# Hybrid decoder trunk, Mamba-2 mixer: gates, norm sums and the first decode rows at later units

## The chip, the cores and the metric

The kernel runs on one core of a Trainium2 chip. The metric is the device time of one execution in microseconds; lower is better. A core has TensorE (matmuls; PE, and PEld for its weight loads), VectorE (DVE), ScalarE (ACT), GpSimd (POOL) and SyncE (SP), each with a queue of its own that it works off in order. Semaphores tie the queues together.

## What is computed

One inference step of a two-layer decoder for a prompt of 256 tokens and 8 decode requests with one token each, which share all weights. The first layer is a half-SwiGLU, a Mamba-2 mixer, a half-SwiGLU and a gated per-layer embedding; the second has windowed attention in place of the mixer. The change touches only the mixer:

```python
def mamba2_mixer(u, w_in, conv_w, conv_b, dt_bias, a_log, d_skip, norm_g, w_out, ssm0, conv0):
    z, xbc, dt_raw = jnp.split(u @ w_in, [D_INNER, D_INNER + CONV_DIM], axis=-1)
    conv = conv_b + sum(xbc_full[:, k:k + t_len] * conv_w[k] for k in range(CONV_W))
    xs, bm, cm = jnp.split(silu(conv), ...)
    y, h_last = ssd_scan(xs, dt, a, bm, cm, ssm0)
    y = y + d_skip * xs
    gated = y * silu(z)                                  # 2048 channels in 8 groups
    gg = gg * rsqrt(mean(gg * gg, over the group) + EPS)
    out = (gg * norm_g) @ w_out
```

## The kernel before

The 264 columns (256 prompt tokens, 8 decode tokens) lie along the free dimension of every tile, features on the 128 partitions. The weights are cut into units of 128 x 1024 values. SP loads them into a ring of four; ACT rounds each to a high part (L982), DVE takes the rest as a low part (L1395), and TensorE makes three products for each of 8 tiles (L435 to L437), 24 matmuls for a unit.

The mixer's input projection has 49 units, numbered s_ = 0 to 48 (list SIN): one for dt, 16 for z, 32 for the convolved channels. Every engine's program runs over the same slots s_ = 0 to 51 (SLOTS), and the lists at L95 to L104 say in which slot a small step is issued. On TensorE the small matmuls of a slot come behind the unit of that slot, in the order of the loop at L870 to L896: add_inter, decode_rows, chunk_in and chunk_out, norm_sums, decode_columns. Each engine only waits for semaphores, so a step's slot is its place in the queue, not a time.

For each of the 8 groups g:
- The scan runs in two chunks of 128 tokens. CHUNK_AT[g] gives the slot. chunk_in (L756, L757) makes the differences of which ACT takes the exponential (L1173, with a table load), DVE multiplies (L1739), chunk_out (L770, L775, L777) uses the product.
- decode_rows (L796) spreads a state row over partitions; ACT copies them (copy_rows, L1180); decode_columns (L811, L813), one slot later, turns them; DVE reads them two slots after the rows (decode_read, L1699 and L1701); POOL finishes (dec_outputs, L2050).
- In slot GATE_AT[g] DVE multiplies y by silu(z) (gate, L1759) and ACT squares it (L1239). In slot NORM_AT[g] POOL adds the two tiles of squares (pair_squares, L2056) and TensorE sums them over the partitions into bank 2 (norm_sums, L827).
- In slot ROOT_AT[0] = NORM_AT[3] ACT takes the square root of the first four groups' sums (L1245, semaphore gated_std); in the next slot DVE inverts it (invert_stats, L1764); two and three slots after the root POOL sends it to DRAM and back, spread over the partitions (stats_out, stats_in). It is used from slot APPLY_AT = 43 on.

Inside a slot, DVE's order is: take the unit from PSUM (L1442), decode_read, the three convolution taps of the unit before (L1643), steps of the chunk, gate, low part of a later unit; in slots without a chunk the low part comes ahead of these; then invert_stats. ACT's order is: high part of a later unit, first tap (L1139), exponential, SiLU of the unit before (L1145 or L1150), copy_rows, square, root.

Decode columns and norm sums write into different columns of PSUM bank 2, from which DVE (decode_read) and ACT (the root) read. The waits in norm_sums and decode_columns keep TensorE from writing while the others read: norm_sums(g) waits until all decode_reads are done whose columns lie in an earlier slot than NORM_AT[g]; decode_columns waits for the root where it comes behind it.

Of the kernel before, what the change touches and what calls it, by code (L numbers as in the profile page):

```python
# [95 lines left out]
DEC_CONV_AT = [e_ + 1 for e_ in LAST_CONV]  # L96
DEC_SILU_AT = [e_ + 2 for e_ in LAST_CONV]
DEC_PROD_AT = [14] + [e_ + 3 for e_ in LAST_CONV[1:]]
DEC_AT = [16, 19, 23, 27, 32, 37, 43, 46]
GATE_AT = [19, 22, 26, 30, 36, 46, 48, 50]  # L100
NORM_AT = [t_ + 1 for t_ in GATE_AT]
ROOT_AT = [NORM_AT[3], NORM_AT[7]]
APPLY_AT = 43
SLOTS = ROOT_AT[1] + 1  # L104
# [44 lines left out]
def trunk_kernel(nc, weights, xT, pT, cst, vec, convst, ssm0, kcT, vc_in, ck, cv,  # L149
# [3 lines left out]
    with ExitStack() as ctx:  # L153
# [275 lines left out]
        def _(pe):  # L429
# [306 lines left out]
            def chunk_in(k):  # L736
# [14 lines left out]
                if c == 1:  # L751
                    pe.wait_ge(dec_copied, [d_ < CHUNK_AT[g] + 1 for d_ in DEC_AT].count(True))
                if k == 0:
# [5 lines left out]
            def chunk_out(k):  # L759

                g, c = k // 2, k % 2
                yb = bank[6]
                pe.wait_ge(ssd_mm, k + 1)
                if k == 0:
                    pe.wait_ge(pre_a, 3)
                if g >= 1 and c == 0:
                    pe.wait_ge(ssd_y, g)

                for h in range(4):
                    pe.matmul(yb[64 * (h % 2):64 * (h % 2) + 64, 256 * (h // 2) + 128 * c:256 * (h // 2) + 128 * c + 128],  # L770
                              xdt[k % 2][:, 64 * h:64 * h + 64], Dm[k % 2][:, 128 * h:128 * h + 128],
                              start=h < 2, stop=c == 0, skip_group_check=True)
                if k > 0:
                    pe.wait_ge(ssd_carry, k)
                mm = pe.matmul(bank[3][:, 0:256], cbb[k % 2][:, 128:256], xte[k % 2], start=True, stop=True)  # L775
                if c == 1:
                    mm = pe.matmul(bank[3][:, 256:512], xact[:, 24 + g, 128:256], h1, start=True, stop=True)  # L777
                mm.then_inc(ssd_part, 1)

            def add_inter(g):  # L780

                pe.wait_ge(ssd_isc, g + 1)
                for n_ in range(2):
                    mm = pe.matmul(bank[6][:, 256 * n_ + 128:256 * n_ + 256], isc[:, 128 * n_:128 * n_ + 128], ident,
                                   start=False, stop=True, skip_group_check=True)
                mm.then_inc(ssd_tr, 1)

            def decode_rows(g):

                pe.wait_ge(h0_landed[H0_BUF[g]], 16 * h0_turn(g))  # L790
                pe.wait_ge(dec_act, g + 1)
                pe.wait_ge(ssd_exp, 2 * [c_ + 1 < DEC_AT[g] for c_ in CHUNK_AT].count(True))
                if g > 0:
                    pe.wait_ge(dec_copied, g)
                for q in range(SEQS):
                    mm = pe.matmul(bank[7][32 * (q % 4):32 * (q % 4) + 32, 256 * (q // 4):256 * (q // 4) + 256],  # L796
                                   dact[:, g, 1, q:q + 1].to_broadcast([P, 32]), h0buf[H0_BUF[g]][:, 256 * q:256 * q + 256], start=True, stop=True)
                mm.then_inc(h0_used, 1)

            def decode_columns(g):  # L800

                pe.wait_ge(dec_copied, g + 1)
                pe.wait_ge(dec_prod, g + 1)
                if g > 0:
                    pe.wait_ge(dec_read, g)
                if DEC_AT[g] + 1 > NORM_AT[3]:
                    pe.wait_ge(gated_std, 1)
                c_ = N + 24 * g
                for i in range(2):
                    for t in range(2):  # L810
                        pe.matmul(bank[2][:, c_ + 8 * t + 4 * i:c_ + 8 * t + 4 * i + 4], crow[:, 256 * i + 128 * t:256 * i + 128 * t + 128],  # L811
                                  ident[:, 0:P:32], start=True, stop=True)
                pe.matmul(bank[2][:, c_ + 16:c_ + 24], ones, bc_d[:, g, :], start=True, stop=True).then_inc(dec_sel, 1)  # L813

            def norm_sums(g):

                if g < G - 1:
                    pe.wait_ge(gated_pair, g + 1)
                else:
                    pe.wait_ge(gated_sq, G)  # L820
                pe.wait_ge(dec_read, [d_ + 1 < NORM_AT[g] for d_ in DEC_AT].count(True))
                if g >= 4:
                    pe.wait_ge(gated_std, 1)
                rows = bank[2][32 * (g % 4):32 * (g % 4) + 32, 0:N]
                tiles = 1 if g < G - 1 else 2
                for k in range(tiles):
                    mm = pe.matmul(rows, ones[:, 0:32], gsq[:, k, :], start=k == 0, stop=k == tiles - 1)  # L827
                mm.then_inc(gated_sum, 1)
# [42 lines left out]
            for s_ in range(len(SIN)):  # L871
                if s_ == 1:
                    unit_pair("sin", 0)
                elif s_ > 1:
                    sin_unit(s_)
                if s_ == PRE_AT:
                    pre_tokens()
                if s_ == PRE_AT + 3:
                    pre_sums()
                for g in range(G):  # L880
                    if s_ == CHUNK_AT[g] + 3:
                        add_inter(g)
                if s_ in DEC_AT:
                    decode_rows(DEC_AT.index(s_))
                for g in range(G):
                    if s_ == CHUNK_AT[g]:
                        chunk_in(2 * g)
                    if s_ == CHUNK_AT[g] + 1:
                        chunk_in(2 * g + 1)
                        chunk_out(2 * g)  # L890
                    if s_ == CHUNK_AT[g] + 2:
                        chunk_out(2 * g + 1)
                if s_ in NORM_AT:
                    norm_sums(NORM_AT.index(s_))
                if s_ - 1 in DEC_AT:
                    decode_columns(DEC_AT.index(s_ - 1))  # L896
# [78 lines left out]
        def _(act):  # L975
# [190 lines left out]
            def decay_exp(k):  # L1166

                if k + 1 < 2 * G:
                    select(k + 1)
                act.wait_ge(ssd_diff, k + 1)  # L1170
                if k >= 2:
                    act.wait_ge(ssd_part, k - 1)
                act.activation(Dm[k % 2], bank[5 + 2 * (k % 2)][:, 0:512], ACT.Exp).then_inc(ssd_exp, 1)  # L1173
# [22 lines left out]
            for s_ in range(SLOTS):  # L1196
# [35 lines left out]
                if s_ in CHUNK_AT[1:]:  # L1232
                    decay_exp(2 * CHUNK_AT.index(s_))
                if s_ in GATE_AT:
                    g = GATE_AT.index(s_)
                    act.wait_ge(gated, g + 1)
# [152 lines left out]
        def _(dve):  # L1389
# [331 lines left out]
            def carry(k):  # L1721

                g, c = k // 2, k % 2
                dve.wait_ge(ssd_part, k + 1)
                if c == 0:
                    dve.tensor_copy(h1, bank[3][:, 0:256]).then_inc(ssd_carry, 1)
                    return
                if g > 0:
                    dve.wait_ge(ssd_tr, g)
                dve.tensor_tensor(by_head(isc), by_head(bank[3][:, 256:512]), heads(tok[:, 1, 0, 4 * g:4 * g + 4]), ALU.mult).then_inc(ssd_isc, 1)  # L1730
                link(dve, dve_step, steps, dve.tensor_tensor(by_head(h1), by_head(h1), heads(tok[:, 1, 2, 4 * g:4 * g + 4]), ALU.mult))
                if g >= 2:
                    dve.wait_ge(st_out[g % 2], 16 * (g // 2))
                dve.tensor_tensor(state[:, g % 2, :], h1, bank[3][:, 0:256], ALU.add).then_inc(ssd_carry, 1)
# [19 lines left out]
            def gate(g):  # L1754

                dve.wait_ge(z_silu, 2 * g + 2)
                dve.wait_ge(dec_y, g + 1)
                dve.wait_ge(ssd_y, g + 1)
                dve.tensor_tensor(zs[:, 2 * g:2 * g + 2, :], zs[:, 2 * g:2 * g + 2, :], xact[:, 2 * g:2 * g + 2, :], ALU.mult).then_inc(gated, 1)  # L1759
# [11 lines left out]
            for s_ in range(SLOTS):  # L1771
# [36 lines left out]
                for g in range(G):  # L1808
# [7 lines left out]
                    if s_ == CHUNK_AT[g] + 2:  # L1816
                        carry(2 * g + 1)
                if s_ in GATE_AT:
                    gate(GATE_AT.index(s_))
                if s_ < len(SIN) and chunks:  # L1820
# [159 lines left out]
        def _(pool):  # L1980
# [72 lines left out]
            def pair_squares(g):  # L2053

                pool.wait_ge(gated_sq, g + 1)
                pool.tensor_tensor(gsq[:, 0, :], gsq[:, 0, :], gsq[:, 1, :], ALU.add).then_inc(gated_pair, 1)  # L2056
# [11 lines left out]
            for s_ in range(SLOTS):  # L2068
                if s_ in NORM_AT[:G - 1]:
                    pair_squares(NORM_AT.index(s_))  # L2070
# [251 lines left out]
```

## Time and profile before

| | us |
|---|---|
| median of three runs | 1239.3 |
| lowest and highest | 1239.04, 1241.94 |
| the profiled execution | 1243.26 |
| span of the profiled execution | 1241.2 |

| engine | busy us |
|---|---|
| TensorE, matmuls | 1206.5 |
| DVE | 885.1 |
| ACT | 689.8 |
| POOL | 233.1 |

The span is the time from the first to the last instruction of the profile. "Busy" counts the time in which an engine has an instruction in work. Idle time of an engine that isn't the bottleneck costs nothing; what counts is where TensorE stands still, and which wait ends last there.

### The profile page before, as it was taken

The page shows a single profiled execution, that of the slowest core. Times are in us where ns is not written, and L with a number is a line of the kernel's source. Part 1 is how long each engine was busy: PE and PEld are TensorE (multiplying, and loading weights), DVE is VectorE, ACT ScalarE, POOL GpSimd, SP SyncE. Part 2 cuts the span into 40 slices and gives each one's busy share as a digit, 9 for nine tenths or more (in the row PEclk, how much of TensorE's full clock was granted, in tenths as well). Part 3 has the DMA queues.
Part 4 walks back from the last instruction along what each step waited for, and adds up shares of the span by engine and source line. Part 5 has one row for each costly group of instructions (what it writes and reads, how often), then busy time and mean ns, then how long its engine had stood idle before and what let it go on. Part 6 is the DMA issues. An engine that isn't in the chain of part 4 may idle for free.

```text
span 1241.2 us, 26732 instructions
## 1 busy us (share of the span) xinstructions
PE 1206.5 (97%) x9875; PEld 1172.5 (94%) x9875; DVE 885.1 (71%) x1405; ACT 689.8 (56%) x1098; POOL 233.1 (19%) x338
## 2 busy tenths in 40 slices
PE   6999999899999999999999999999999999999998
PEld 6999999888888889999999999999998899999998
DVE  5666646987888777786744988788469758776447
ACT  6444436676576547556555764555357656445335
POOL 0000002312222111132344333332015310000001
PEclk9999999999999999999999999999999899999999
DMA  7655554644443445857686666756743135455552
GB/s 265 230 207 182 185 178 153 227 157 177 143 158 134 149 136 189 333 193 278 242 316 224 213 239 222 263 190 226 247 166 105 56 136 199 175 185 184 173 184 87
DMA packets 61424, 239.08 MB, mean 193 GB/s; under 512 B 7080, under 2 KB 8272, under 8 KB 56976
## 3 DMA queue, kind: packets, MB, share of 16 engines
q1 hardware_dynamic: 55008, 197.01, 45.6%
q0 software_dynamic: 6064, 40.66, 9.2%
q8 instruction: 42, 0.69, 0.2%
q10 hardware_dynamic: 288, 0.54, 0.1%
q14 instruction: 22, 0.18, 0.0%
HBM read 226.87 MB, written 13.39 MB: 194 GB/s over the span
## 4 chain that ended last, share of the span: by engine, by line
PE 75%; DVE 13%; ACT 6%; issue 4%; DMA 1%; POOL 0%; DVEq 0%; SPq 0%; ACTq 0%
PE bank L435 24%; PE bank L436 23%; PE bank L437 23%; DVE wlo L1395 4%; ACT whi L982 2%; DVE xact L1643 1%; DVE xl L1414 1%; ACT L1173 1%; DVE x L1425 1%; DVE rstd L1436 1%; DVE gu L1442 1%; DMA x<-xT 1%; DMA xact<-stat_rows 1%; POOL gsq L2056 0%; PE bank L467 0%
## 5 line engine op out<-in xcount | busy, mean ns | idle before, releaser
L1395 DVE TENSOR_TENSOR wlo<-raw,whi 128x1024 fp32r<-128x1024 f32 x369 | 459.7, 1249 | 254.8 <-ACT whi L982 253.5
L435 PE MATMUL bank<-xh,whi 128*128 128x264 f32 x2024 | 584.6, 289 | 16.1 <-DVE xl L1414 11.8
L436 PE MATMUL bank<-xl,whi 128*128 128x264 f32 x2024 | 577.0, 285 | 0.0
L437 PE MATMUL bank<-xh,wlo 128*128 128x264 f32 x2024 | 576.6, 285 | 0.0
L982 ACT ACTIVATE whi<-raw 128x1024 fp32r<-128x1024 f32 x369 | 387.4, 1054 | 258.0 <-PE bank L437 245.0
L435 PEld LDWEIGHTS bank<-xh,whi 128*128 128x128 f32 x2024 | 384.6, 190 | 21.4 <-issue 14.2
L436 PEld LDWEIGHTS bank<-xl,whi 128*128 128x128 f32 x2024 | 384.7, 190 | 0.9
L437 PEld LDWEIGHTS bank<-xh,wlo 128*128 128x128 f32 x2024 | 382.9, 189 | 0.0
L435 PE MATMUL bank<-hh,whi 128*128 (+1 forms) x896 | 256.0, 286 | 2.0 <-DVE xact L1510 0.9
L437 PE MATMUL bank<-hh,wlo 128*128 (+1 forms) x896 | 255.1, 285 | 0.0
L436 PE MATMUL bank<-hl,whi 128*128 (+1 forms) x896 | 254.4, 284 | 0.0
L435 PEld LDWEIGHTS bank<-hh,whi 128*128 128x128 f32 x896 | 168.6, 188 | 3.9 <-issue 1.5
L436 PEld LDWEIGHTS bank<-hl,whi 128*128 128x128 f32 x896 | 169.1, 189 | 0.1
L437 PEld LDWEIGHTS bank<-hh,wlo 128*128 128x128 f32 x896 | 168.6, 188 | 0.0
L1049 ACT ACTIVATE hh<-gu 128x264 fp32r<-128x264 f32 (+1 forms) x88 | 37.4, 425 | 168.3 <-DVE gu L1454 168.3
L1990 POOL TENSOR_TENSOR sq<-sq 128x264 f32<-128x264 f32 x49 | 39.3, 801 | 457.2 <-ACT sq L1020 451.9
L1442 DVE TENSOR_TENSOR gu<-bank,rstd 128x264 f32<-128x264 f32 x192 | 82.0, 429 | 16.6 <-PE bank L437 14.9
L1459 DVE TENSOR_TENSOR hl<-gu,hh 128x264 f32 (+1 forms) x88 | 45.2, 514 | 28.9 <-ACT hh L1049 28.9
L2126 POOL TENSOR_TENSOR xact<-xact,da_bc 128x512 f32<-128x512 f32 x32 | 40.6, 1268 | 100.9 <-PE bank L437 93.8
L1643 DVE SCALAR_TENSOR_TENSOR xact<-under,vs,xact 128x256 f32<-128x256 f32 x96 | 47.2, 492 | 2.3
L1454 DVE TENSOR_TENSOR gu<-gu 128x264 f32<-128x264 f32 x88 | 44.9, 510 | 0.2 <-ACT gu L1044 0.2
L2131 POOL TENSOR_TENSOR xact<-xact 128x512 f32<-128x512 f32 x20 | 31.2, 1561 | 58.2 <-PE bank L437 58.2
(309 smaller groups left out, 996.9 us busy)
## 6 DMA issues: line engine op xcount, KB each, us to landing
raw<-weights SPq DMA_DIRECT2D x369, 512.0 KB, 3.5
under<-ssm POOLq DMA_DIRECT2D x8, 1024.0 KB, 7.5
xact<-ssm POOLq DMA_DIRECT2D x8, 1024.0 KB, 7.7
out_ssm_s<-xact POOLq DMA_DIRECT2D x8, 1024.0 KB, 5.0
xact<-dtx_rows POOLq DMA_DIRECT2D x5, 1024.0 KB, 10.8
zs<-dtx_rows POOLq DMA_DIRECT2D x2, 1024.0 KB, 14.7
x<-xT SPq DMA_DIRECT2D x2, 528.0 KB, 7.0
xact<-stat_rows POOLq DMA_DIRECT2D x2, 528.0 KB, 6.4
```

Of the source, the lines that this page charges most:

```text
L435: pe.matmul(out, whi[:, w, c], rh, start=start, stop=False)
L436: pe.matmul(out, whi[:, w, c], rl, start=False, stop=False)
L437: return pe.matmul(out, wlo[:, w, c], rh, start=False, stop=stop)
L982: act.activation(whi[:, s, :], raw[:, s, :], ACT.Copy).then_inc(hi_ready, 1)
L1049: act.activation(dst, gu[:, 2 * p + 1, :], ACT.Copy).then_inc(hh_ready, 1)
L1395: dve.tensor_tensor(wlo[:, s, :], raw[:, s, :], whi[:, s, :].bitcast(F32), ALU.subtract).then_inc(lo_ready, 1)
L1442: dve.tensor_tensor(dst, src[:, 0:N], rstd[:, :], ALU.mult).then_inc(a_free, 1)
L1454: dve.tensor_tensor(gu[:, 2 * p + 1, :], gu[:, 2 * p, :], gu[:, 2 * p + 1, :], ALU.mult).then_inc(h_ready, 1)
L1459: dve.tensor_tensor(one(hl), gu[:, 2 * p + 1, :], one(hh).bitcast(F32), ALU.subtract).then_inc(hl_ready, 1)
L1643: dve.scalar_tensor_tensor(out=out, in0=xr[:, k:k + T], scalar=vs[:, V_CW + CT * k + c:V_CW + CT * k + c + 1], in1=out, op0=ALU.mult, op1= ...
L1990: pool.tensor_tensor(sq3[:, 0, :], sq3[:, 0, :], sq3[:, m, :], ALU.add).then_inc(sq_pair, 1)
L2126: pool.tensor_tensor(by_head(part), by_head(part), da_bc[:, 2 * k:2 * k + 2, 4 * q:4 * q + 4].unsqueeze(3).to_broadcast([P, 2, 4, 64]), AL ...
```

## The change

The gates (and squares) of groups 0 to 4 are issued one slot later, the POOL addition and the norm sums of these groups two slots later. As ROOT_AT and SLOTS are computed from NORM_AT, the first root moves from slot 31 to 33, and what hangs on it moves too. The decode rows of group 0 move from slot 16 to 17. A comparison in decode_columns includes equality, so that columns in the slot of the fourth norm sums wait for the root as well.

```diff
-DEC_AT = [16, 19, 23, 27, 32, 37, 43, 46]
-GATE_AT = [19, 22, 26, 30, 36, 46, 48, 50]
-NORM_AT = [t_ + 1 for t_ in GATE_AT]
+DEC_AT = [17, 19, 23, 27, 32, 37, 43, 46]
+GATE_AT = [20, 23, 27, 31, 37, 46, 48, 50]
+NORM_AT = [t_ + 2 for t_ in GATE_AT[:5]] + [t_ + 1 for t_ in GATE_AT[5:]]
 ROOT_AT = [NORM_AT[3], NORM_AT[7]]
...
-                if DEC_AT[g] + 1 > NORM_AT[3]:
+                if DEC_AT[g] + 1 >= NORM_AT[3]:
                     pe.wait_ge(gated_std, 1)
```

## Rows read from the trace of the kernel before

**Rows 1.** The page: busy time of each engine, share of the span, instructions.

```profile
PE 1206.5 (97%) x9875; PEld 1172.5 (94%) x9875; DVE 885.1 (71%) x1405; ACT 689.8 (56%) x1098; POOL 233.1 (19%) x338
```

**Rows 2.** TensorE's waits from 265 to 445 us: total, times, longest.

```profile
PE bank L827 <- POOL gsq L2056: 5.6, 7, 1.4
...
PEld bank L827 <- POOL gsq L2056: 8.1, 7, 1.6
```

**Rows 3.** Weight loads in time (start, length, idle before): norm sums 0 to 4.

```profile
294.58 0.14 PEld L827 LDWEIGHTS bank<-gsq,cs 128*32 128x32 f32 x2 [0.83 <-POOL gsq L2056]
295.14 0.97 PEld L811 LDWEIGHTS bank<-cs,under 128*128 128x128 f32 x8 [0.42 <-issue]
...
312.41 0.14 PEld L827 LDWEIGHTS bank<-gsq,cs 128*32 128x32 f32 x2 [0.95 <-POOL gsq L2056]
...
333.07 0.14 PEld L827 LDWEIGHTS bank<-gsq,cs 128*32 128x32 f32 x2 [0.97 <-POOL gsq L2056]
...
351.59 0.14 PEld L827 LDWEIGHTS bank<-gsq,cs 128*32 128x32 f32 x2 [1.47 <-POOL gsq L2056]
...
380.69 0.14 PEld L827 LDWEIGHTS bank<-gsq,cs 128*32 128x32 f32 x2 [0.95 <-POOL gsq L2056]
```

**Rows 4.** Timelines of TensorE and DVE: decode rows, product and chunk_out of slot 16.

```profile
271.67 0.62 PEld L796 LDWEIGHTS bank<-under,dact 128*32 128x32 f32 x16 [2.44 <-issue]
272.70 0.41 PEld L770 LDWEIGHTS bank<-sq 128*64 128x64 f32 x8 [0.41 <-DVE sq L1739]
...
271.59 0.69 DVE L1739 TENSOR_TENSOR sq<-sq,under 128x512 f32<-128x512 f32 x1 [1.88 <-ACT sq L1173]
```

**Rows 5.** Timelines: TensorE begins units 29 and 30; DVE takes unit 29 and reads.

```profile
338.08 0.19 PEld L435 LDWEIGHTS bank<-xh,whi 128*128 128x128 f32 x1
...
340.99 0.19 PEld L435 LDWEIGHTS bank<-xh,whi 128*128 128x128 f32 x1
...
341.40 0.43 DVE L1442 TENSOR_TENSOR zs<-bank,rstd 128x264 f32<-128x264 f32 x1 [0.72 <-PE bank L437]
...
341.84 0.17 DVE L1701 TENSOR_TENSOR gu<-bank,da_d 128x16 f32<-128x16 f32 x1
```

**Rows 6.** Weight loads of slot 33: add_inter, columns of group 4, then unit 34.

```profile
360.59 0.53 PEld L784 LDWEIGHTS bank<-cs,under 128*128 128x128 f32 x4
361.04 0.97 PEld L811 LDWEIGHTS bank<-cs,under 128*128 128x128 f32 x8
...
362.16 0.19 PEld L435 LDWEIGHTS bank<-xh,whi 128*128 128x128 f32 x1
```

**Rows 7.** Timelines of DVE and ACT: reciprocal, taps and SiLU of unit 32; root.

```profile
360.27 1.80 DVE L1764 RECIPROCAL gu<-gu 128x264 f32<-128x264 f32 x1
...
362.27 1.51 DVE L1643 SCALAR_TENSOR_TENSOR xact<-under,vs,xact 128x256 f32<-128x256 f32 x3
...
354.44 1.28 ACT L1245 ACT_TABLE_LOAD   x1
355.73 0.48 ACT L1245 ACTIVATE gu<-bank,cs 128x264 f32<-128x264 f32 x1
...
363.82 0.42 ACT L1145 ACTIVATE xact<-xact 128x256 f32<-128x256 f32 x1 [0.83 <-DVE xact L1643]
```

**Rows 8.** DVE's takes of units 34 and 35; chunk_out(10) on TensorE.

```profile
365.62 0.42 DVE L1442 TENSOR_TENSOR zs<-bank,rstd 128x264 f32<-128x264 f32 x1
...
368.80 0.42 DVE L1442 TENSOR_TENSOR under<-bank,rstd 128x264 f32<-128x264 f32 x1
...
373.32 0.42 PEld L770 LDWEIGHTS bank<-sq 128*64 128x64 f32 x8 [0.36 <-DVE sq L1739]
```

**Rows 9.** Windows: PE, PEld, DVE, ACT, POOL busy; then granted clock, DMA share, GB/s.

```profile
235.00:240.00 5.00, 2.43 (x20) 2.25 (x20) 4.86 (x10) 3.54 (x6) 1.30 (x4) 1.00 0.36 119
240.00:245.00 5.00, 5.00 (x31) 5.00 (x30) 4.93 (x12) 3.07 (x6) 0.97 (x2) 0.66 0.86 302
...
269.00:272.00 3.00, 0.75 (x12) 0.50 (x14) 1.12 (x4) 2.96 (x5) 0.00 (x0) 1.00 0.54 182
```

## The prediction

> **What bounds the kernel now.** I read the page first: TensorE is busy 97% of the span [rows 1], so a change pays only where TensorE stands still. All that is moved lies in the mixer's input projection, between about 265 and 445 us. So I next read who waits there [rows 2]: no matmul of a unit waits for its weights; TensorE waits for small things, above all for the POOL addition in front of the norm sums. Third I laid TensorE's weight loads in order of time and counted units by their 24 loads; one unit takes 2.9 us (338.08 to 340.99) [rows 5], and each slot (unit number s_) is followed by its small matmuls. That gives the idle time at each of the first five norm sums [rows 3]: 0.83, 0.95, 0.97, 1.47 and 0.95 us, 5.2 in sum. Last I read the DVE and ACT rows of the slots that the code makes wait for each other after the change. The profiled execution spans 1241.2 us and took 1243.26, 4.0 above the median of 1239.3; the sum below is a difference to that span, and I add it to the median.
>
> **What the lists say.** NORM_AT goes from 20, 23, 27, 31, 37 to 22, 25, 29, 33, 39; the gates and their squares come one slot later, the POOL addition and the sums two. ROOT_AT[0] goes from 31 to 33, the reciprocal on DVE with it from slot 32 to 34, the two DMAs of the statistics from 33 and 34 to 35 and 36. The first decode rows go from slot 16 to 17, their columns to 18, their read to 19. Three conditions in the code change with the lists:
> (a) norm_sums(g) waits for every decode_read whose columns lie in an earlier slot. Before, the newest such read lay two slots back or more. After, for g = 1, 2 and 4 it lies in DVE's own slot 25, 29, 39, the slot of the sums.
> (b) decode_columns(4) lies in slot 33, right behind norm_sums(3), and waits for gated_std, the square root that ACT takes in slot 33 from just these sums. Before, the root lay two slots earlier.
> (c) chunk_in(3) in slot 18 waits for ACT's copy of the decode rows of slot 17, one slot back instead of two.
>
> **Waits removed.** With one unit more between gate and sums, gate, square and addition are hidden under a unit, also where DVE lags by half a unit. Not all 5.2 us go: a change of matmul shape leaves a gap of its own, 0.42 us behind the sums, 0.36 to 0.41 between other small matmuls [rows 3, 4, 8]. I take 0.15 to 0.2 at four places and 0.4 behind chunk_in in slot 25, 1.1 together: 4.1 us saved. Bounds: 3.6 (over all seven POOL waits the matmuls stood still 5.6 us and the loads 8.1; that share of 5.2) and 5.2 [rows 2, 3]. The sums themselves cost the same.
>
> **Decode rows of the first group.** They stall 2.4 us for the exponential of chunk 1 and run at 271.67, while DVE's product for chunk_out(1) runs from 271.59 to 272.2; chunk_out(1) follows at 272.70 [rows 4]. Moved out, chunk_out(1) starts at about 272.3, since it waits for that product: 0.4 us saved, not 2.4. The rows ran in that shadow; in slot 17 they stand in the open, 1.2 us with both gaps. The copy of the rows on ACT now lies in slot 17 ahead of the exponential of chunk 2, for which chunk_out(2) waits: another 0.1, an estimate. Sum +0.9 us. Bounds: -0.4 if the rows in slot 17 fill a wait, +1.2. The POOL load of the next state comes one slot later and is not needed before slot 27: nothing; condition (c) has over 1 us to spare: nothing, a few tenths if ACT is late.
>
> **New waits for decode reads.** In slot 29 nothing lies between the unit and the sums. DVE starts its take of unit 29 0.4 us after TensorE went on to unit 30, and the read ends at 342.0, 1.0 us after unit 30 began [rows 5]. That is the wait if DVE keeps its distance: 0.9 us. In slot 25 chunk_in lies in between and the read is done in time: 0, bound 0.3. In slot 39 it is 0.9, and 1.3 if DVE still lags by what comes below; I take 1.3. Together 2.2 (0.9 to 3).
>
> **The wait for the root.** First how far TensorE is from the old trace, step by step: +0.9 after slot 18, -0.6 after 20, +0.2 after 22 (sums and gap, 0.8), -1.3 after 23, -0.6 after 25 and the wait of chunk_out in 26, -2.1 after 27, -0.4 after 29, and -2.4 after slot 31 (sums, gap and wait gone). DVE and ACT start slot 30 with TensorE, 0.4 early, and then work nearly without a pause, so they stay at 0.4. The sums of slot 33 then end near 359.5: in the old trace the columns start at 361.04 [rows 6], less 2.4, plus 0.7 for the sums and some 0.15 of gap. ACT reaches the root only behind the SiLU of unit 32, and this waits for DVE's three taps of unit 32. Before, the reciprocal of 1.80 us at 360.27 stood ahead of them, the taps began at 362.27 and the SiLU at 363.82 [rows 7]. Without the reciprocal (1.72 net of overlap) and 0.4 earlier the SiLU starts at about 361.7 and ends at 362.1. Then the table load, 1.28, and the root, 0.48 [rows 7]: ready at 363.9. TensorE waits 4.4 us. Behind it on TensorE's queue stand the columns of group 4 and every further unit; unit 34, at 362.16 before [rows 6], starts at about 365.0. Bounds: 1.9 (ACT at the root when the sums end) and 5.0. In the trace the table load starts as soon as the activation ahead of it ends. The Trainium skill (ScalarE: Activation LUTs, "What ACT_TABLE_LOAD costs") adds a drain of about 1.38 us to each change of table; by that the wait would be near 5.8 us, but the root row follows the load at once, and I stay with the row.
>
> **The reciprocal in slot 34.** It now stands in the way of the take of unit 35. In the old trace 3.18 us lie between the takes of units 34 and 35 on DVE [rows 8]; with 1.72 more it is 4.9, while TensorE needs 2.9. The exponential of chunk 10 waits for ACT's tap of that unit, and chunk_out(10) started with no reserve (0.36, the bare gap) [rows 8]. So 1.15 us more (0 to 1.6). In slot 32 it had cost nothing. The statistics' rows are read in slot 43: their later DMAs cost nothing.
>
> **Sum.** -4.1 + 0.9 + 2.2 + 4.4 + 1.1 = +4.5 us.
>
> **TensorE's clock.** In the trace the granted clock fell behind such a pause: TensorE stood still for 2.6 of the 5 us from 235 to 240, and the granted clock over 240 to 245 was 0.66, so 3.4 us of it were at the lower level (1.2 GHz in place of 2.4) and cost 1.7. In 269 to 272, with 2.3 us of pause, it stayed at 1.00 [rows 9]. A pause of 4.4 us is longer than both. I take a drop with +1.5 us (0 if it falls into waits). The Trainium skill (TensorE: Matmul & The Clock Gate, "HAM oscillation — how this bites in real kernels") says that work after a long wait starts at the halved clock; the first pause agrees, the second shows none. With the drop the difference is +6.0: 1247.2 of span, 1245.3 against the median.
>
> **Rivals.**
> - The same without a clock drop: +4.5, 1243.8. For it the pause at 269 us, against it the one before 240.
> - ACT is at the root when the sums end, since DVE gets ahead with the earlier units: the wait is 1.9, the reciprocal costs 0.5, the reads 0.9: -4.1 + 0.9 + 0.9 + 1.9 + 0.5 = +0.1, about 1239.4. For it: DVE is free of the gate in slots 19, 22, 26. Against: from slot 30 on the gate moves within the busy stretch, and the taps of unit 32 have no reserve.
> - Faster: the taps and the SiLU of slot 33 end over 2 us before the sums do, so that the root follows the sums within 0.7 us, the reads hide, and the rows of slot 17 fall into a wait (-0.4): -4.1 - 0.4 + 0.7 = -3.8, 1235.5. It decides from the point where DVE is less than half a unit behind TensorE in slots 30 to 33; it starts slot 30 at that distance, and the sum above puts TensorE 2 us further ahead by slot 33.
> - The change doesn't do what it says: the sums still wait for POOL, because DVE reaches the gates later by as much as TensorE gains. Then nothing is saved at two or three of them and the rest stays: about +8, 1247.5. Against it: the old waits are 1 to 1.5 us [rows 3], and a unit more gives 2.9.
>
> **How the numbers follow.** Forecast with clock drop 0.48; without 0.2; root wait short 0.17; faster 0.09; no saving 0.06. The low end goes down to the third case, 1239.0; the high end takes the longer root wait and both reads with the drop, 1249.0. A measurement tells about 0.3% (3.7 us) from no change: the limits are 1235.6 and 1243.0. Slower: nearly all of the first and last case, two thirds of the second: 0.64. Faster 0.09. Within 0.3%: 0.27.
>
> **What the changed profile would show.** Right: no POOL wait before the first five sums; a pause of 4 to 5 us on TensorE before the group-4 columns behind the sums of slot 33, ended by ACT's square root; waits near 1 us before the sums of slots 29 and 39, ended by DVE; chunk_out(10) waiting over 1 us; the first decode rows without a stall, but chunk_out(1) with one near 3 us; unit 34 some 3 us later than 362.16; a stretch at the lower clock right behind. Wrong: a root that starts within 1 us of the sums' end, or sums that still wait for POOL; then the distance of DVE and ACT to TensorE, on which all of it rests, was misjudged.

## The result, and the profile after

The changed kernel takes 1251.24 us (median of 4 runs, 1248.94 to 1251.68) beside 1240.62 of the kernel before (4 runs, 1239.04 to 1242.61): ratio 1.0078, 95% interval 1.0064 to 1.0092. It is slower, as forecast, but by 9.7 us by the ratio (10.6 between the two medians) against the forecast 6.0, and the median lies 2.2 us above the upper end of the range. The profiled execution took 1250.81 us with a span of 1248.7 (before: 1243.26 and 1241.2).

The page after, busy time by engine, answers to [rows 1]:

```profile
PE 1208.1 (97%) x9875; PEld 1173.7 (94%) x9875; DVE 887.5 (71%) x1405; ACT 690.3 (55%) x1098; POOL 233.8 (19%) x338
```

No engine has more instructions; TensorE is busy 1.6 us longer with the same 9875. TensorE's waits from 265 to 445 us, total, times and longest, answer to [rows 2]:

```profile
PE bank L770 <- DVE sq L1739: 5.2, 4, 2.9
PE bank L811 <- ACT gu L1245: 4.7, 1, 4.7
PE bank L827 <- POOL gsq L2056: 2.3, 2, 1.4
PE bank L827 <- issue: 1.5, 1, 1.5
PE bank L827 <- DVE gu L1701: 0.9, 1, 0.9
```

The waits for POOL fell from seven to the two of groups 5 and 6, which the change doesn't touch. In their place stand one wait of 4.7 us of the columns of group 4 (L811) for the square root (L1245), and two of the sums for the decode read (L1701; the one told as "issue" is the wait of slot 39). The weight loads of the sums of groups 0, 2 and 4 and of slot 33, where the sums of group 3 now lie (start, length, idle before in brackets), answer to [rows 3] and [rows 6]:

```profile
306.38 0.14 PEld L827 LDWEIGHTS bank<-gsq,cs 128*32 128x32 f32 x2 [0.33 <-issue]
...
340.82 0.14 PEld L827 LDWEIGHTS bank<-gsq,cs 128*32 128x32 f32 x2 [1.06 <-issue]
...
359.72 0.14 PEld L827 LDWEIGHTS bank<-gsq,cs 128*32 128x32 f32 x2
365.04 1.78 PEld L811 LDWEIGHTS bank<-cs,under 128*128 128x128 f32 x8 [5.18 <-issue]
...
367.13 0.33 PEld L435 LDWEIGHTS bank<-xh,whi 128*128 128x128 f32 x1
...
397.03 0.14 PEld L827 LDWEIGHTS bank<-gsq,cs 128*32 128x32 f32 x2 [1.71 <-issue]
```

Between the sums and the columns TensorE loads no weights for 5.18 us (its matmuls stand still for 4.7, since the matmuls of the sums run on behind their load), and unit 34 starts at 367.13 instead of 362.16. The first loads behind the pause are slow: the eight of the columns take 1.78 us (0.97 before), one load of the unit 0.33 (0.19). What it waited for is in the timelines of DVE and ACT, which answer to [rows 7]:

```profile
361.17 1.52 DVE L1643 SCALAR_TENSOR_TENSOR xact<-under,vs,xact 128x256 f32<-128x256 f32 x3
...
362.72 0.42 ACT L1145 ACTIVATE xact<-xact 128x256 f32<-128x256 f32 x1 [0.83 <-DVE xact L1643]
363.15 1.28 ACT L1245 ACT_TABLE_LOAD   x1
364.45 0.48 ACT L1245 ACTIVATE gu<-bank,cs 128x264 f32<-128x264 f32 x1
...
372.07 1.07 ACT L982 ACTIVATE whi<-raw 128x1024 fp32r<-128x1024 f32 x1 [7.14 <-PE bank L437]
```

The chain is the one of the prediction: taps of unit 32, SiLU, table load, root, columns. The root ends at 364.93 and the columns follow. The last row is the other side of the pause: ACT then has 7.14 us with nothing to do (DVE 7.41), because no unit ends in that time. The windows answer to [rows 9] (busy time of PE, PEld, DVE, ACT, POOL, then the granted clock, DMA share, GB/s):

```profile
270.00:275.00 5.00, 3.48 (x16) 2.79 (x17) 4.15 (x9) 4.25 (x8) 1.09 (x4) 0.68 0.25 86
...
360.00:365.00 5.00, 0.36 (x2) 0.00 (x0) 4.53 (x8) 3.31 (x5) 0.90 (x2) 0.90 0.54 206
365.00:370.00 5.00, 4.93 (x23) 4.96 (x24) 0.00 (x0) 0.00 (x0) 0.00 (x0) 0.50 0.57 210
370.00:375.00 5.00, 4.95 (x38) 4.74 (x37) 2.91 (x7) 2.79 (x4) 1.89 (x5) 0.92 0.01 3
```

A granted clock of 0.50 over a whole window is the lower level, 1.2 GHz. TensorE is at it for nearly 7 us, from 364 to 371, the end of the pause and the work behind it, and for another stretch in slots 16 and 17. That second one lies behind chunk_out(1), which answers to [rows 4] without the decode rows ahead of it:

```profile
271.52 0.48 PEld L770 LDWEIGHTS bank<-sq 128*64 128x64 f32 x8 [3.10 <-DVE sq L1739]
...
278.13 0.59 PEld L796 LDWEIGHTS bank<-under,dact 128*32 128x32 f32 x16
```

Last, the reciprocal and what it delays, which answer to [rows 8]:

```profile
375.20 1.79 DVE L1764 RECIPROCAL gu<-gu 128x264 f32<-128x264 f32 x1
376.92 0.36 DVE L1442 TENSOR_TENSOR under<-bank,rstd 128x264 f32<-128x264 f32 x1
...
381.33 0.42 PEld L770 LDWEIGHTS bank<-sq 128*64 128x64 f32 x8 [1.64 <-DVE sq L1739]
```

DVE takes unit 35 only behind the reciprocal, and TensorE idles 1.64 us in place of 0.36 before chunk_out(10).

### The profile page after: what moved, and what is told of

Same layout as the page of the kernel before. It is cut to its first block, busy times and chain, and to the rows that moved or that the text cites. A ratio compares the mean times of both kernels' runs of the same rounds, so it can differ in the third digit from the quotient of the medians.

```text
span 1248.7 us, 26732 instructions
## 1 busy us (share of the span) xinstructions
PE 1208.1 (97%) x9875; PEld 1173.7 (94%) x9875; DVE 887.5 (71%) x1405; ACT 690.3 (55%) x1098; POOL 233.8 (19%) x338
## 4 chain that ended last, share of the span: by engine, by line
PE 75%; DVE 14%; ACT 6%; issue 3%; DMA 1%; DVEq 0%; POOL 0%; SPq 0%; ACTq 0%
PE bank L435 23%; PE bank L436 23%; PE bank L437 23%; DVE wlo L1395 4%; ACT whi L982 2%; DVE xact L1643 1%; DVE xl L1414 1%; ACT L1173 1%; DVE x L1425 1%; DVE rstd L1436 1%; DMA x<-xT 1%; DVE gu L1442 1%; DMA xact<-stat_rows 1%; PE bank L775 0%; DVE under L1442 0%
```

## Where the time went, unit by unit

I laid the starts of the units of both traces side by side, aligned at unit 14, ahead of all that is moved. The shift (after minus before, us) at some units, with the forecast of the prediction:

| start of unit | 18 | 20 | 21 | 24 | 28 | 32 | 34 | 40 |
|---|---|---|---|---|---|---|---|---|
| measured | 1.2 | 2.4 | 1.0 | 0.2 | -0.6 | -0.8 | 5.8 | 9.8 |
| less the slow stretch of slots 16, 17 (1.6) | -0.4 | 0.8 | -0.6 | -1.4 | -2.2 | -2.4 | 4.2 | 8.2 |
| forecast | -0.4 | 0.9 | -0.6 | -1.3 | -2.1 | -2.4 | 2.8 | 6.0 |

The forecast at 40 is the sum with its clock drop; at 34 it is 365.0 less 362.16. Up to unit 32 the steps came out to a tenth. The gap opens in slot 33, with the clock. From 9.8 to the 7.5 us between the two spans: the old trace is already 0.8 behind at unit 14 (257.20 and 256.38), after its slow stretch of [rows 9], and at 427 to 432 it has another one of 1.5, which this execution of the new kernel lacks.

The theories tested: **A**, the wait for the root in slot 33 with the lower clock behind it and the reciprocal in slot 34 make the loss. **B**, the waits for decode reads in slots 29 and 39 (and what they delay) make it. **C**, the slow stretches come by chance and have nothing to do with the pause. **D**, the decode rows in slot 17 are a gain, or cost nothing.

## The experiments

All are medians against runs of the kernel before (1240.62 us over 4 runs beside the change, 1241.82 over 29 beside the first four experiments, 1241.85 over 23 beside the second four). The ratio isn't the ratio of the two medians, and can differ from it by 0.1%. "Clock loss" is summed from windows of 2 us over the whole profiled execution, as (1 - granted clock) x 2 us for each window below 0.99. In the old kernel's trace it is 8.5 us, so its span without it is 1232.7. Time in which TensorE stands still counts in this loss too, so the last column is good to one or two us.

| run | median us | ratio, 95% interval | span | clock loss | span less loss |
|---|---|---|---|---|---|
| the change | 1251.24 | 1.0078, 1.0064 to 1.0092 | 1248.7 | 10.2 | 1238.5 |
| columns ahead of the sums | 1242.20 | 1.0005, 0.9997 to 1.0014 | 1240.9 | 8.5 | 1232.4 |
| decode rows back in 16 | 1248.47 | 1.0060, 1.0047 to 1.0073 | 1246.4 | 10.3 | 1236.1 |
| decode rows alone | 1242.36 | 1.0005, 0.9997 to 1.0014 | 1240.2 | 6.8 | 1233.4 |
| group 3 stays, rows in 16 | 1241.36 | 0.9996, 0.9987 to 1.0004 | 1236.5 | 3.4 | 1233.1 |
| sums alone, one later | 1239.28 | 0.9984, 0.9975 to 0.9992 | 1235.6 | 5.1 | 1230.5 |
| the same, group 3 at 32 | 1239.92 | 0.9983, 0.9973 to 0.9992 | 1238.7 | 8.5 | 1230.2 |
| the change, reciprocal in 39 | 1246.26 | 1.0041, 1.0027 to 1.0056 | 1246.0 | 10.2 | 1235.8 |
| group 3 alone | 1249.82 | 1.0070, 1.0057 to 1.0083 | 1247.2 | 11.9 | 1235.3 |

### Columns of group 4 ahead of the sums (e1)

On top of the change. In slot 33 the columns no longer stand behind the sums, and so need not wait for the root; DVE's read of these columns waits for the root instead, so that it doesn't read bank 2 while TensorE writes the sums. In short:

```
 (TensorE, slot ROOT_AT[0])
-norm_sums(3)
 decode_columns(4)
+norm_sums(3)
-if DEC_AT[g] + 1 >= NORM_AT[3]:      (decode_columns waits for gated_std)
+if DEC_AT[g] + 1 > NORM_AT[3]:
 (DVE, decode_read)
+if DEC_AT[g] + 1 == NORM_AT[3]: dve.wait_ge(gated_std, 1)
```

> The changed kernel with one order turned: in slot 33 TensorE issues the decode columns of group 4 ahead of the fourth norm sums, so that it never waits for the root; DVE's read of these columns waits for it instead. Theory A (the root wait in slot 33, 4.7 us on TensorE, and the lower clock behind it are most of the loss, with the reciprocal in slot 34): 5 to 7 us faster than the changed kernel, so +3 to +6 us against the kernel before; no wait before L811 in slot 33, no stretch at the lower clock in slots 33 to 35. Rival B (the loss comes from the sums waiting for decode reads and the later gates): stays within 2 us of the changed kernel, +8 to +11 against before. Rival C (the stretches at the lower clock come at random and carry the difference): the pause goes, the time falls by 4.7 at most and lower-clock stretches appear elsewhere in the mixer as often.

The ratio falls from 1.0078 to 1.0005. The slot in the loads of this kernel:

```profile
358.71 0.97 PEld L811 LDWEIGHTS bank<-cs,under 128*128 128x128 f32 x8
359.92 0.14 PEld L827 LDWEIGHTS bank<-gsq,cs 128*32 128x32 f32 x2
```

and the windows behind it:

```profile
360.00:365.00 5.00, 5.00 (x39) 4.58 (x40) 4.87 (x12) 3.76 (x6) 1.38 (x4) 1.00 0.70 239
365.00:370.00 5.00, 4.82 (x38) 4.52 (x38) 4.96 (x8) 3.65 (x7) 2.19 (x6) 1.00 0.71 260
```

No pause, no slow stretch behind it, the columns at their old 0.97. The two waits for decode reads, 0.9 and 1.5 us, are unchanged. The reciprocal is in slot 34 in this kernel too, and it still holds up the take of unit 35 and chunk_out(10):

```profile
366.94 1.79 DVE L1768 RECIPROCAL gu<-gu 128x264 f32<-128x264 f32 x1
368.65 0.36 DVE L1444 TENSOR_TENSOR under<-bank,rstd 128x264 f32<-128x264 f32 x1
...
373.07 0.42 PEld L770 LDWEIGHTS bank<-sq 128*64 128x64 f32 x8 [1.57 <-DVE sq L1743]
```

The idle time is 1.57 us, beside 1.64 in the change and 0.36 before. So the reciprocal in this slot costs its 1.2 us with the pause or without it. With the pause goes nearly the whole loss all the same: by the ratio 0.6 us are left, where 3 to 6 had been expected, and unit 40 starts 7.4 us earlier against the kernel before than in the change. The pause and the clock behind it are the loss, and B falls as its main cause; the reciprocal, the reads and the rows together are about what the POOL waits taken away give back.

### Decode rows back in slot 16 (e2), and decode rows alone (e3)

```
-DEC_AT = [17, 19, ...]      (e2, on top of the change)
+DEC_AT = [16, 19, ...]
-DEC_AT = [16, 19, ...]      (e3, on the kernel before)
+DEC_AT = [17, 19, ...]
```

> The changed kernel with the first decode rows back in slot 16. Theory A: the rows fill a wait there; moving them cost 1.1 us and, through the longer pause (3.1 instead of 2.4 us), a stretch at the lower clock of 1.3 us; so 1 to 2.5 us faster than the changed kernel, +8 to +9.5 against before. Rival D (moving the rows saved its 2.3 us wait and the loss is all elsewhere): 2 us slower than the changed kernel, +12 to +13.

> The kernel before with only the first decode rows moved to slot 17. Theory A: +1.1 us without and +2.4 us with a stretch at the lower clock behind the pause in slot 16, whose weight-load idle grows from 2.4 to about 3.1 us. Rival D: 2 us faster than before.

With the rows back the kernel is still at 1.0060, 7.4 us above the kernel before, a little under the expected 8 to 9.5. At unit 40 its shift is 7.4 instead of 9.8; 1.6 of the difference is the slow stretch of slots 16 and 17, which it lacks, and 0.8 are the rows. The rows alone measure 1.0005; in their trace they cost 0.96 us at unit 19, steady at 0.55 to 0.58 from unit 21 on. The stall didn't go with them:

```profile
271.56 0.42 PEld L770 LDWEIGHTS bank<-sq 128*64 128x64 f32 x8 [3.11 <-DVE sq L1739]
...
276.55 0.59 PEld L796 LDWEIGHTS bank<-under,dact 128*32 128x32 f32 x16
```

2.44 us ahead of the rows became 3.11 ahead of chunk_out(1), as forecast; the rows had run in the time of DVE's product. D falls as far as a gain of 2 us is meant. The traces show a cost of 0.57 to 0.96 us, 0.9 forecast; the timed ratio alone can't tell it from no cost, since its interval holds both. It is a small part of the change.

### Group 3 stays (e4)

On top of the change, with the decode rows in slot 16: the gate and sums of group 3, the root and the reciprocal at their old places; groups 0, 1, 2 and 4 as in the change.

```
-DEC_AT = [17, ...]    GATE_AT = [20, 23, 27, 31, 37, ...]    NORM_AT = [22, 25, 29, 33, 39, ...]
+DEC_AT = [16, ...]    GATE_AT = [20, 23, 27, 30, 37, ...]    NORM_AT = [22, 25, 29, 31, 39, ...]
```

> The changed gates and sums for groups 0, 1, 2 and 4, but group 3 (gate 30, sums 31, root 31, reciprocal 32) and the first decode rows as before. Theory A: no root wait; about 0.5 us saved at each of groups 0 and 1, group 2 and 4 gain 0.8 and lose 0.9 to the decode read in their slot: -1 us against before, between -2 and +0.5. Rival B: the waits for decode reads carry the loss, +3 us or more against before.

0.9996: B's waits are there (0.9 and 1.5 us) and the loss is not. But neither is the gain of the four POOL waits taken away; the shift is -3.0 at unit 28 and -0.3 at unit 40. That is where B's waits cost. The wait of 1.5 us in slot 39 is there though the reciprocal is back in slot 32.

### The sums alone, one unit later (f5)

On the kernel before: no gate is moved, the sums of groups 0, 1, 2 and 4 lie two slots behind it, group 3 and the rows as they were. No decode read lies in the slot of the sums.

```
-NORM_AT = [t_ + 1 for t_ in GATE_AT]
+NORM_AT = [22, 24, 28, 31, 38, 47, 49, 51]
```

> The kernel before with only the sums moved, to slots 22, 24, 28, 31, 38: gates, root, first decode rows unmoved, and never in the slot of a decode read. Theory A (each old POOL wait is worth its 0.8 to 1.5 us less the gap of the matmul shape, and the new losses come from the slots with a decode read): no POOL wait at groups 0, 1, 2, 4, one of 1.5 us at group 3, unit 41 about 3.0 us earlier against unit 14 than before; -2 to -4 us in the time. Rival E (sums behind their gate are hidden whatever the slot, because DVE and ACT are the bound in the mixer and take the gain back): less than 1 us.

0.9984, and the interval leaves 1 out: 2.0 us faster than the kernel before by the ratio, 2.5 by the shift at unit 41. That is less than 0.3%, but 12 runs beside 23 tell it. Its waits of TensorE from 265 to 445 us:

```profile
PE bank L827 <- POOL gsq L2056: 3.3, 3, 1.4
PE bank L796 <- ACT sq L1173: 2.3, 1, 2.3
PE bank L770 <- DVE sq L1739: 1.1, 2, 0.6
```

No wait for a decode read, and unit 41 starts 2.3 us earlier against the kernel before than in e4. The two kernels also differ in the slots of four gates; with that said, the two reads cost about 2.3 us, and e4's own waits for them add up to 2.4. The term of the prediction was 2.2.

### The same with group 3 at 32 (f6)

The sums and root of group 3 one slot later too, and the rows of group 4 in slot 33, so that their columns are clear of the root.

```
-DEC_AT = [16, 19, 23, 27, 32, ...]    NORM_AT = [22, 24, 28, 31, 38, ...]
+DEC_AT = [16, 19, 23, 27, 33, ...]    NORM_AT = [22, 24, 28, 32, 38, ...]
```

> The same with the fourth sums and the root at slot 32 and the decode rows of group 4 at slot 33, so that the columns behind the root come at slot 34, two slots after it. Theory A: the POOL wait of group 3 goes too, and TensorE doesn't wait for the root: another 1.2 us, about -4.2 at unit 41, -3 to -5 us in the time. Rival F (the root on ACT and the reciprocal on DVE, one slot later than before, hold up chunk 10 as in the changed kernel): no better than with group 3 unmoved, with a wait of about 1 us at L770 in slot 36.

0.9983, no better than f5, though the POOL wait of 1.47 us is gone. The chunk_out(9) of this kernel:

```profile
353.21 0.42 PEld L770 LDWEIGHTS bank<-sq 128*64 128x64 f32 x8 [1.35 <-DVE sq L1739]
...
354.86 0.14 PEld L827 LDWEIGHTS bank<-gsq,cs 128*32 128x32 f32 x2 [0.33 <-issue]
```

Before, it stood behind the rows of group 4 with 0.41 of idle. The rows had filled a wait for DVE's product, and moved out they leave it open, as in slot 16. The saving I had put on this run was lost there: the same mistake that I had avoided for group 0. The shift at unit 41 is -0.7, or -2.3 without the slow stretch in slot 16 that this execution has, where -4.2 was expected. chunk_out(10) idles 0.56 in this kernel, not the microsecond more that rival F had put there: the reciprocal in slot 33, one slot later than before, costs 0.2. In slot 34 it costs 1.2, with the pause (the change) and without it (e1).

### The reciprocal later (f7)

On top of the change: the reciprocal of slot 34 goes to slot 39, its DMAs to 40 and 41.

```
-if s_ - 1 == ROOT_AT[0]: invert_stats(0)
+if s_ - 6 == ROOT_AT[0]: invert_stats(0)
-ROOT_AT[0] + 2: stats_out(0)    ROOT_AT[0] + 3: stats_in(0)
+ROOT_AT[0] + 7: stats_out(0)    ROOT_AT[0] + 8: stats_in(0)
```

> The changed kernel with the reciprocal in slot 39 instead of 34 and the two DMAs of the statistics in slots 40 and 41. Theory A: chunk_out(10) in slot 36 no longer waits beyond the gap of 0.36 us, so 1.2 us less than the changed kernel; the sums of slot 39 still wait 1.5 us for the decode read. Rival G: the take of unit 35 was late because of the clock and the pause, not the reciprocal: L770 in slot 36 still waits over 1 us.

```profile
363.77 1.78 PEld L811 LDWEIGHTS bank<-cs,under 128*128 128x128 f32 x8 [5.19 <-issue]
...
378.63 0.42 PEld L770 LDWEIGHTS bank<-sq 128*64 128x64 f32 x8 [0.36 <-DVE sq L1739]
...
394.09 0.14 PEld L827 LDWEIGHTS bank<-gsq,cs 128*32 128x32 f32 x2 [1.47 <-issue]
```

The pause is the same, the idle time of chunk_out(10) is back at 0.36: the reciprocal cost 1.27 (1.15 forecast). The ratio is 1.0041 in place of 1.0078. The ratios give it 4.6 us where the trace gives 1.3 for the reciprocal. This execution also had no slow stretch in slot 16 (1.6); the rest of some 1.7 us stays open, and with intervals of 1.4 us to either side of both ratios it may be noise. The weight load of the sums of slot 39 still idles 1.47 us beside 1.71 in the change (their matmuls 1.3 beside 1.5): most of this wait is not the reciprocal's lag.

### Group 3 alone (f8)

On the kernel before: only the gate of group 3 in slot 31 and its sums in 33, with the condition of the root.

```
-GATE_AT = [19, 22, 26, 30, 36, ...]    NORM_AT = [20, 23, 27, 31, 37, ...]
+GATE_AT = [19, 22, 26, 31, 36, ...]    NORM_AT = [20, 23, 27, 33, 37, ...]
-if DEC_AT[g] + 1 > NORM_AT[3]:
+if DEC_AT[g] + 1 >= NORM_AT[3]:
```

> The kernel before with only group 3 moved as in the change: gate 31, sums and root 33, reciprocal 34, and the columns of group 4 waiting for the root. Theory A: saved 2.0 us in slot 31, lost 0.8 for the sums in slot 33, 5.7 for the root, 1.7 to 2.5 for the lower clock behind it and 1.2 for the reciprocal: +7 to +8.5 us against before, nearly all of the change's loss. Rival B (the loss needs the other four moves too): under +4.

```profile
363.67 1.78 PEld L811 LDWEIGHTS bank<-cs,under 128*128 128x128 f32 x8 [5.19 <-issue]
...
379.98 0.42 PEld L770 LDWEIGHTS bank<-sq 128*64 128x64 f32 x8 [1.62 <-DVE sq L1739]
```

1.0070: this one group makes the loss of nearly the whole change, 8.7 of 9.7 us, with the same pause and the same wait in slot 36. It is just above the expected 7 to 8.5. The rest of the change, one good part (the POOL waits) and two bad ones (rows and reads), about cancels, which e4 (0.9996) says from the other side. A holds.

## The clock behind the pause

C can be judged by counting. A slow stretch of some 7 us lies right behind the wait for the root in all four traces with that wait (the change at 364 to 371, e2, f7, f8), and in none of the six without (before, e1, e3, e4, f5, f6). C falls there. By the windows each costs 3.4 us, but part of the stretch passes while TensorE still stands (in the change from 364.0 to the first load at 365.0). What falls on work in the change is 2.6 us: 1.0 in the columns (from their first load to unit 34 it is 2.09 us in place of 1.12) and 1.7 in unit 34, whose 24 loads take 4.64 us (367.13 to 371.77) in place of 2.97.

In slot 16 it is otherwise. Behind 3.1 us of idle the clock fell in the change and in e1 and didn't in e3 and f7; behind 2.4 us it fell in f6 and f8 and didn't in before, e2, e4 and f5. The windows 272 to 275 of f6, and of e3 with the longer pause:

```profile
272.00:275.00 3.00, 3.00 (x16) 2.41 (x11) 2.93 (x7) 2.29 (x6) 1.09 (x4) 0.52 0.34 105
```

```profile
272.00:275.00 3.00, 3.00 (x25) 2.75 (x21) 2.93 (x6) 2.28 (x6) 1.10 (x4) 1.00 0.21 71
```

The longer pause kept the clock, the shorter lost it. What decides it isn't shown by these traces; for a forecast it is chance, at 1.6 us a time. For these shorter pauses, then, C isn't refuted. It can be one source of the spread of one kernel's runs (1240.6 to 1243.9 in e1), and it is why the spans of single executions here must be read less their clock loss. Whether the decode rows in slot 17 make the fall more frequent (2 of 4 against 2 of 6) stays open.

## Why the prediction was right and wrong

- **POOL waits taken away, -4.1.** Right: all five are gone, and the shifts of -1.5, -1.5 (unit 24), -1.5 (unit 28) and -2.0 (unit 32) are those forecast. f5 shows for groups 0, 1, 2 and 4 that this part alone is a gain, 0.6 to 0.7 us net a group.
- **Decode rows, +0.9.** Right for the time without the clock: 0.96 at unit 19 in e3. The clock in slots 16 and 17 was left out of it; [rows 9] showed 1.00 behind a pause of 2.3 us, and one trace was no proof that it always is so.
- **Decode reads, +2.2.** Right in sum (2.3, e4 against f5), right in slot 29 (0.9). In slot 39 it was 1.5, not 1.3, and for the most part not for the reason given: without the reciprocal in slot 34 it is 1.5 in e4 and 1.3 in f7. In e4 DVE goes to the take of unit 39 without a pause, where it had waited 0.6 us for TensorE before: it is late there by itself.
- **Wait for the root, +4.4.** The mechanism, the order on DVE and ACT and the place are right; it is 4.7. The root followed its table load by 0.02 us (363.15 + 1.28 = 364.43; 364.45), with no drain between. By the Trainium skill (ScalarE: Activation LUTs, "What ACT_TABLE_LOAD costs"), which adds a drain of about 1.38 us to a change of table, the wait would have been about 5.8 us. The trace doesn't agree: no such time stands ahead of the load or behind it.
- **Reciprocal, +1.15.** Right: 1.27 (f7). e1 has it without the pause too, 1.2 us, so it was right to add the two as terms of their own.
- **Clock, +1.5: the step that failed.** It took the price of the one slow stretch of [rows 9] (1.7 us behind 2.6 us of standing still) for the price behind a wait of 4.4 us, and put no drop at all at slot 16. Behind the measured wait of 4.7 us the stretch was twice as long, 6.8 us, and 2.6 us were lost on work. With the stretch in slots 16 and 17, 1.6, the clock took 4.2 us in this trace where 1.5 stood. The other 1.1 us of the shift at unit 40 (9.8 against 6.0) are small ones behind unit 32: root 0.3, reciprocal 0.1, some 0.4 in slots 37 to 39, and 0.3 spread over slots 32 to 35.
- **What the old trace held besides.** The trace of the kernel before held stretches of both lengths, which the prediction didn't read. Near 978 us, in the second layer, the clock is at the lower level for 6.8 us:

```profile
975.00:980.00 5.00, 5.00 (x75) 4.97 (x71) 2.39 (x9) 2.17 (x9) 0.90 (x3) 0.77 0.19 71
980.00:985.00 5.00, 5.00 (x31) 3.98 (x29) 2.82 (x10) 0.84 (x2) 4.23 (x9) 0.55 0.16 52
```

  TensorE is busy throughout there, so this row gives no price of a pause either; but it shows that 3.4 us was not the longest stretch to reckon with.
- **The range.** Its upper end took the longer waits with the drop at its one price. These terms give 1246.7 and all upper bounds together 1248.0; no term leads to the 1249.0 that was written. A pause longer than any in the mixer's old trace needed an upper bound of the clock term above the one price seen. With 4.2 in its place the sum is 8.7, and 1239.3 plus 8.7 is 1248.0, still within the range. What took the result out of it is the base as well: the three runs of the old kernel had a median of 1239.3, the four beside the change 1240.6 (the same three and one more), the 52 later ones 1241.8. A forecast made as median plus difference carries the error of a median of three, 1 to 2.5 us here, and the range had left it out.
- **The rivals.** The short root wait (the columns waited 4.7 us), the faster case and the unsaved POOL waits all fell, each by the row that the prediction named for it. The case without a clock drop, put at 0.2, fell as well: the drop came behind this wait in all four traces that have it.

## What to carry to other kernels

Before a step is moved to hide a wait, ask who waits for its result and what stands on that engine's queue behind the waiter: here five waits of a microsecond each were hidden at the price of one that held the whole unit loop. A small step that runs beside a wait is free only there; moved out, it costs its own time and the wait stays (slot 16, and slot 32 in f6). A pause of TensorE can cost more than its length (here 4.7 us and 2.6 more), and the surcharge of a longer pause must not be taken from a shorter one. The better version of this change moves only the sums, and no group whose result others wait for (f5, 0.16% faster than the kernel before).

## What was not expected of the hardware

- The length of the slow stretch behind a pause: some 3.4 us behind 2.6 of standing still [rows 9], 6.8 us behind the 4.7 us of the wait for the root, in all four traces that have it. Behind 2.4 to 3.1 us of idle in slot 16 a stretch of 3.4 us came in 4 of 10 traces; behind the same pause of 2.6 us near 237 us it came in nine of the ten, and not in the change's. That the length follows the pause isn't shown: the 6.8 us near 978 us stand behind none.
- The Trainium skill (TensorE: Matmul & The Clock Gate, "HAM oscillation — how this bites in real kernels") has work after a long wait start at the halved clock. The traces agree behind the wait for the root (5.2 us without a weight load), every time; behind the pauses of 2.4 and 3.1 us in slot 16 they agree in four of ten and not in the other six.
- A slow stretch needs no change nearby: near 427 to 440 us the clock is at 0.89 over 15 us in the old kernel, e1, e3, f6, f7 and f8, and at 1.00 in the change, e2, e4 and f5. What decides it stays open. The row of the old kernel:

```profile
425.00:440.00 15.00, 13.15 (x88) 11.67 (x89) 12.30 (x27) 7.23 (x13) 2.36 (x5) 0.89 0.34 113
```
